# Gate and query projections: four jobs of four 128-row blocks with a 512-column product of high weights and split activations, in place of eight jobs of two blocks

## The reference

```
for l in (0, 1):                                   # two "mla" layers
    shift, scale, gate = split(silu(c) @ w_ada[l] + b_ada[l], 3)
    h = layernorm(x) * (1 + scale) + shift
    u_f, z_f, cq, ckv, k_r, z_a = split(h @ w_in[l])
    y_f = fourier_mix(u_f, w_fmix[l]) * silu(z_f)
    q  = rmsnorm(cq) @ w_q_b[l];  k, v = rmsnorm(ckv) @ w_kv_b[l];  rope on parts of q and k
    y_a = attention(q, k, v) * silu(z_a)           # 8 heads of 128
    x = layernorm(alpha * x + gate * (concat(y_f, y_a) @ w_out[l])) * g + b
# "even" layer
p_in, p_gate, dq, dk, dv, d_gate, iq, ik, iw = split(rms_norm(x) @ even_w_in)
score = sum_h relu(iq_h . ik) * iw_h;  the 64 best keys of each query are kept
x = x + concat(silu(p_gate) * pool(p_in), silu(d_gate) * attention(dq, dk, dv, kept keys)) @ even_w_out
# "odd" layer
q, k, v, gate = split(rms_norm(x) @ odd_w_in)      # 32 query heads of 64, a window of 128 tokens
x = x + (silu(gate) * window_attention(q, k, v)) @ odd_w_out
```

## Time and profile before

| what | value |
|---|---|
| device time, median of 3 runs | 1576.37 us |
| lowest and highest of the 3 runs | 1575.11, 1579.06 us |
| span of the profiled execution | 1576.4 us |
| PE busy | 1505.3 us, 95% |
| DVE busy | 1064.3 us, 68% |
| ACT busy | 708.5 us, 45% |
| mean granted TensorE clock, as a share of 2.4 GHz | 0.988 |
| transfers | 345.04 MB, mean 219 GB/s |

### The profile page before, as it was taken

How to read it: one execution, slowest core, us unless ns; L and a number is a source line. 1 busy time by engine, 2 the same in 40 slices (tenths; PEclk the granted TensorE clock), 3 DMA queues, 4 the chain that set the end, 5 groups by cost and what they waited for, 6 DMA issues and landing times.

```text
span 1576.4 us, 25483 instructions
## 1 busy us (share of the span) xinstructions
PE 1505.3 (95%) x10143; PEld 1332.0 (84%) x10143; DVE 1064.3 (68%) x1729; ACT 708.5 (45%) x1216; POOL 40.7 (3%) x58
## 2 busy tenths in 40 slices
PE   5999999989979999999979999999998999999999
PEld 3678789987869788998859998889987998888987
DVE  3348588889987667577576683795655657766653
ACT  2334244334445445444435444454444546655442
POOL 3000000000000000000000000010000000000000
PEclk9999999999989999999999999999999999999999
DMA  9998888998837555776645554456664554434673
GB/s 356 406 407 305 277 292 316 358 351 331 332 100 263 188 192 180 253 251 205 199 151 183 171 166 144 146 181 196 188 197 148 162 160 122 123 118 134 188 219 102
DMA packets 101422, 345.04 MB, mean 219 GB/s; under 512 B 11216, under 2 KB 21684, under 8 KB 100536
## 3 DMA queue, kind: packets, MB, share of 16 engines
q1 hardware_dynamic: 96888, 327.42, 61.7%
q0 software_dynamic: 4416, 16.00, 3.0%
HBM read 341.17 MB, written 2.20 MB: 218 GB/s over the span
## 4 chain that ended last, share of the span: by engine, by line
PE 72%; DVE 12%; DMA 7%; ACT 5%; issue 4%; SPq 1%; DVEq 0%; ACTq 0%
PE PM L1478 60%; PE PB L1478 7%; DMA stg<-in_w_in 5%; DVE wlo L2181 2%; ACT whi L1862 2%; DVE AC L2094 2%; ACT AR L1862 2%; PE PB L1713 1%; DVE X L2094 1%; DMA stg<-in_w_ada 1%; DMA stg<-in_w_out 1%; SPq L1387 1%; PE PB L1685 1%; DVE SM L2444 1%; PE PB L1788 1%
## 5 line engine op out<-in xcount | busy, mean ns | idle before, releaser
L2181 DVE TENSOR_TENSOR wlo<-stg,whi 128x1024 fp32r<-128x1024 f32 (+2 forms) x417 | 498.0, 1204 | 346.4 <-ACT whi L1862 344.4
L1862 ACT ACTIVATE whi<-stg 128x1024 fp32r<-128x1024 f32 (+2 forms) x417 | 430.0, 1039 | 440.7 <-PE PM L1478 336.0
L1478 PE MATMUL PM<-Hh,whi 128*128 128x256 f32 x1824 | 527.9, 292 | 12.6 <-DVE wlo L2181 8.5
L1478 PE MATMUL PM<-Hh,wlo 128*128 128x256 f32 x1776 | 500.1, 284 | 0.0
L1478 PE MATMUL PM<-Hl,whi 128*128 128x256 f32 x1824 | 496.5, 284 | 0.0
L1478 PEld LDWEIGHTS PM<-Hh,whi 128*128 128x128 f32 x1824 | 351.8, 193 | 31.2 <-issue 16.3
L1478 PEld LDWEIGHTS PM<-Hh,wlo 128*128 128x128 f32 x1776 | 342.8, 193 | 0.0
L1478 PEld LDWEIGHTS PM<-Hl,whi 128*128 128x128 f32 x1824 | 341.4, 192 | 0.8 <-issue 0.2
L1478 PE MATMUL PM<-whi,Hh 128*128 128x512 f32 (+1 forms) x576 | 224.8, 391 | 0.9 <-DVE wlo L2181 0.5
L1478 PE MATMUL PM<-wlo,Hh 128*128 128x512 f32 (+1 forms) x576 | 221.4, 385 | 0.0
L1478 PE MATMUL PM<-whi,Hl 128*128 128x512 f32 (+1 forms) x576 | 218.9, 385 | 0.0
(11 more groups left out here) (279 smaller groups left out, 1420.1 us busy)
## 6 DMA issues: line engine op xcount, KB each, us to landing
stg<-in_w_ada SPq DMA_DIRECT2D x163, 512.0 KB, 6.2
stg<-in_w_in SPq DMA_DIRECT2D x105, 512.0 KB, 5.3
stg<-in_even_w_in SPq DMA_DIRECT2D x80, 512.0 KB, 3.6
stg<-in_odd_w_in SPq DMA_DIRECT2D x72, 512.0 KB, 3.5
stg<-in_w_out SPq DMA_DIRECT2D x64, 512.0 KB, 4.0
stg<-in_even_w_out SPq DMA_DIRECT2D x32, 512.0 KB, 3.6
stg<-in_odd_w_out SPq DMA_DIRECT2D x32, 512.0 KB, 3.6
AR<-in_w_ada SPq DMA_DIRECT2D x29, 512.0 KB, 15.1
```

The lines of the kernel that those rows point to most:

```text
L1478: return e.matmul(out, l, r, start=start, stop=stop, skip_group_check=True)
L1862: return e.activation(out, x, f, **k)
L2181: e.tensor_tensor(wlo[s["slot"]][:, :, 0:n], stg[s["slot"]][:, :, 0:n], whi[s["hi"]][:, :, 0:n].bitcast(F32), ALU.subtract).then_inc(SEM[" ...
```

## The change

Gate groups, the query groups of the odd layer, those of the even layer and its second group of iq go from `group` to `wide`. `wide` makes four jobs of 256 output columns; a job holds four blocks of 128 rows. `Hh` and `Hl` of a block now lie side by side in `H2`, so that one matmul of 512 columns computes whi·Hh and whi·Hl into the two halves of a bank; wlo·Hh, with 256 columns, goes to the left half. A pair of banks then holds two blocks of columns, and its right halves have to be added to the left ones: ScalarE copies the two right halves to SBUF and VectorE adds. Of the handlers in the diff `wide` is TensorE's, the next three are ScalarE's and the last two VectorE's.

```diff
+    def wide(self, w, c0, post, pre=None):
+        g = {}
+        for q in range(4):
+            def body(job, q=q):
+                if q == 0:
+                    g["pair"], g["free"] = self.pairs.get()
+                tok = self.tick("mm")
+                self.step("wide", q=q, pair=g["pair"], free=g["free"] if q == 0 else (), split=job["split"], hi=job["hi"],
+                          slot=job["slot"], h=self.h[4 * q:4 * q + 4])
...
+            self.jobs.append(dict(mode="split", src=[(0, 256, w, 4 * q, c0)], n=512, mm=body, pre=pre if q == 0 else None,
+                                  post=done if q == 3 else None))
...
-    def gate_post(self, l, blocks):
+    def gate_post(self, l, b0):
...
-            for j in range(2):
-                b0 = blocks[2 * j]
-                self.drain(lambda: self.z[b0] is not None and self.z[b0 + 1] is not None)
-                i, ifree = self.now(self.tmps)
...
+            i, ifree = self.now(self.tmps)
+            r, total = self.tick("right_half"), self.tick("half_sum")
+            self.step("gate_sum", tmp=i, tfree=ifree, pair=pair, mm=mm, r=r)
+            self.round()
+            self.drain(lambda: self.z[b0] is not None and self.z[b0 + 1] is not None)
+            th, pr, y = self.tick("gate_tanh"), self.tick("gate_in"), self.tick("gate_y")
+            self.step("gate", b0=b0, tmp=i, pair=pair, total=total, th=th, pr=pr, z=[self.z[b0], self.z[b0 + 1]])
+            return [pr]
...
+    def two_out(self, pair, mm, dst, free):
+        r = self.tick("right_half")
+        self.step("two_out", pair=pair, mm=mm, dst=dst, free=free, r=r)
+        return self.tick("half_sum")
...
-        for j in range(4):
-            self.group([(w, j * 512, 512)], A4, q_post(j))
-        for j in range(4):
-            self.group([(w, 2560 + j * 512, 512)], A4, self.gate_post(l, list(range(4 * j, 4 * j + 4))))
+        for j in range(8):
+            self.wide(w, j * 256, q_post(j))
+        for g in range(8):
+            self.wide(w, 2560 + g * 256, self.gate_post(l, 2 * g))
...
+        H2 = sb("H2", [128, KT, 2, S], F32R)
+        Hh, Hl = H2[:, :, 0, :], H2[:, :, 1, :]
...
+                elif kind == "wide":
+                    q.wait_all(s["free"])
+                    q.wait_ge(s["split"])
+                    wh, wl = four(whi[s["hi"]]), four(wlo[s["slot"]])
+                    for kk in range(4):
+                        k = 4 * s["q"] + kk
+                        q.wait_ge(s["h"][kk])
+                        for j in range(2):
+                            b, cols = PM[2 * s["pair"] + j], slice(j * 128, j * 128 + 128)
+                            mm(b, wh[:, kk, cols], H2[:, k, :, :].rearrange("p t n -> p (t n)"), k == 0, False)
+                            ins = mm(b[:, 0:S], wl[:, kk, cols], Hh[:, k, :], False, k == KT - 1)
...
                 elif kind == "gate":
-                    q.wait_ge(s["mm"])
-                    q.wait_all(s["tfree"])
-                    act(TMP[s["tmp"]][:, :], (P0, P1)[s["j"]][:, :], ACT.Tanh, scale=0.5).then_inc(SEM["gate_tanh"], 1)
+                    q.wait_ge(s["total"])
+                    act(two(TMP[s["tmp"]][:, :]), halves(s, 0), ACT.Tanh, scale=0.5).then_inc(SEM["gate_tanh"], 1)
+                elif kind == "gate_sum":
+                    q.wait_ge(s["mm"])
+                    q.wait_all(s["tfree"])
+                    act(two(TMP[s["tmp"]][:, :]), halves(s, 1)).then_inc(SEM["right_half"], 1)
+                elif kind == "two_out":
+                    q.wait_ge(s["mm"])
+                    q.wait_all(s["free"])
+                    act(two(ar(s["dst"], 512)), halves(s, 1)).then_inc(SEM["right_half"], 1)
...
+                elif kind == "gate_sum":
+                    q.wait_ge(s["r"])
+                    q.wait_ge(s["mm"])
+                    e.tensor_tensor(halves(s, 0), halves(s, 0), two(TMP[s["tmp"]][:, :]), ALU.add).then_inc(SEM["half_sum"], 1)
+                elif kind == "two_out":
+                    x = two(ar(s["dst"], 512))
+                    q.wait_ge(s["r"])
+                    q.wait_ge(s["mm"])
+                    e.tensor_tensor(x, halves(s, 0), x, ALU.add).then_inc(SEM["half_sum"], 1)
```

More of the change, by code:

```diff
@@ L736, in heads @@
                 self.z[8 + h + n] = a
[L738 to L741, removed]
+        for g in range(8):
+            self.wide(w, (1024 if g < 4 else 1856) + g * 256, self.gate_post(l, 2 * g))
         return begin
@@ L868, in even, with iq_first @@
         qr = {}
+        def iq_first(pair, mm):
+            for m in range(2):
+                Tk["iq", m] = self.tick("iq_out")
+            self.step("iq_out", pair=pair, mm=mm, dst=IQ, free=tuple(arf))
+            return [Tk["iq", 1]]
         def iq_post(j):
             def post(pair, mm):
[L872 to L875, removed]
+                Tk["iq", j] = self.two_out(pair, mm, IQ + 2 * j * S, tuple(arf))
+                return [Tk["iq", j]]
             return post
-        self.group([(w, 4224, 512)], A4, iq_post(0))
+        self.group([(w, 4224, 512)], A4, iq_first)
         def ik_post(pair, mm):
@@ L900, in even @@
                    [unit("A", 0, 0, 0), unit("A", 1, 0, 128, 80)], ik_post)
[L901 removed]
+        for j in (2, 3):
+            self.wide(w, 4224 + j * 256, iq_post(j))
         def scores():
@@ L939, in post @@
             def post(pair, mm):
[L940 to L943, removed]
+                a = self.two_out(pair, mm, Q2 + 2 * j * S, tuple(arf))
+                Tk["q", 2 * j] = Tk["q", 2 * j + 1] = a
                 return [a]
             return post
-        for j in range(2):
-            self.group([(w, 2048 + j * 512, 512)], A4, q_post(j))
+        for j in range(4):
+            self.wide(w, 2048 + j * 256, q_post(j))
         def p_post(j):
@@ L984, in even @@
             self.group([(w, j * 512, 512)], B2, p_post(j), pre=q_rinv if j == 0 else None)
[L985 to L988, removed]
+        for g in range(8):
+            self.wide(w, (1024 if g < 4 else 2176) + g * 256, self.gate_post(l, 2 * g))
         return begin
@@ L1015, in post @@
             def post(pair, mm):
[L1016 to L1021, removed]
+                a = self.two_out(pair, mm, IQ + 2 * j * S, tuple(arf))
+                Tk["q", 2 * j] = Tk["q", 2 * j + 1] = a
+                if j % 2:
+                    g = j // 2
+                    self.start(self.head_rinv(4, IQ + 4 * g * S, {("q", k): Tk["q", 4 * g + k] for k in range(4)}, 80 + 16 * g, qr[g]))
+                    self.start(heads(g))
                 return [a]
```

51 lines of the change are left out of this document (31 added, 20 removed).

## The result

The changed kernel takes 1595.81 us (median of 4 runs, 1592.07 to 1598.74). The kernel before, run beside it on the same chip, takes 1576.45 us (4 runs, 1575.11 to 1579.06). The ratio is 1.0115, 95% interval 1.0095 to 1.0135: slower, by 19.4 us at the medians. The forecast was 1573.6 us, its range 1560 to 1587. The profiled execution of the changed kernel took 1592.07 us, of which its span is 1590.3; in every execution that gives both, 1.75 to 2.24 us lie outside the span. So the span before, 1576.4 us, does not equal the median because nothing lies outside of it: that agreement was chance, worth some 2 us.

A forecast was written before the change was run, and what follows sets the result against it. PE was taken to bound the clean gate stretches, VectorE and loads layer 0, VectorE and ScalarE much of the odd attention, the even layer between. 1576.4 - 12.9 (PE gain) + 10.1 (costs) = 1573.6 us, range 1560 to 1587.

The forecast's parts named there:

- What is added: All layers: costs of the added copies, additions and waits, 10.1 us in sum.
- What bounds the kernel: PE alone in layer 1's gates; VectorE and loads in layer 0; VectorE and ScalarE mostly in odd attention; even layer between.
- That part once per three matmuls: Wide streams: 13.3 ns beside a matmul's columns saved once per three matmuls, 0.42 us a piece.
- A gate piece costs VectorE 0.69 of work plus about 0.7 of standing still = 1.4 us: Each gate piece: VectorE's addition plus its wait for the tanh, 1.4 us.
- Its copies cost nothing as long as the next `whi` is not late: ScalarE, everywhere: it has room, so added copies cost nothing, else 0.6 us each.
- I take the middle, 6.4: Layer 0: seven gate pieces cost between 3.1 and 9.8 us, depending on VectorE's usable idle time; 6.4 us taken.
- Odd attention: ... 2.8 us: Odd layer's attention: three gates cost 4.2 us, of which the chain's non-PE share, 2/3, passes on: 2.8 us.
- 2 x 1.4 x 1/3 = 0.9: Even layer: two gates cost 0.9 us; its six other additions nothing, or 1.4 us.
- I price this at nothing, the work being the same: Gate pieces: one more call of `round` each makes attention steps slightly denser; no cost.
- VectorE's round trip multiplies in layer 0: Rival, 20%: layer 0's standing delays slot releases and loads, a gate costs 1.4 + 2.35 us; 1593 us, or 1585.
- The pair of banks is not free in time: Rival, 5%: in attention stretches, queue waits hold the banks, 15 mixed pieces with 1 us each; 1589 us.
- A matmul's fixed part is not saved: Rival, 6%: the mixed stream keeps four fifths of the 13.3 ns, the gain is 2.6 us; 1583.9 us.

The follow-up runs named there:

- experiment 1: The changed kernel without the extra call of round between the sum and the gate; 1591.05 us.
- experiment 3: The changed kernel without extra round, gates' copies and all additions, so right halves are never added; 1567.02 us.
- experiment 5: The changed kernel without extra round; in each gate piece the tanh and two VectorE steps behind it issued one weight job later; 1575.02 us.
- 13: As experiment 5, with the 14 queries' additions also issued one weight job after their copies; 1571.03 us.
- form 11: The changed kernel without extra round; copy, addition and tanh at once, only the two VectorE steps behind the tanh one job later; 1589.56 us.
- experiment 6: The changed kernel without extra round and without the gates' 32 ScalarE copies; additions add the tile's old content; 1590.54 us.
- Form 9: The changed kernel without extra round; the whole gate (copy, addition, tanh, two steps) issued in one piece, one job later; 1586.10 us.
- 14: As 13, but layer 0's gates stay in groups of 512 columns as before; 1572.16 us.
- experiment 4: Only the 14 query and iq pieces wide; gates in groups as in the kernel before, no extra round; 1577.11 us.
- 12: As form (10), with the 14 queries' additions also issued one job after their copies; 1575.92 us.
- experiment 2: The kernel before with one more call of round after the fourth and eighth job of each gate group, nothing wide; 1583.84 us.
- form (10): As experiment 5, cut once more: gate copy at the piece's end, addition one job later, tanh and two steps another job later; 1580.68 us.

## Why the prediction was wrong

The step that failed is "What is added", the sum of costs: 10.1 us were said, and the runs show 24.0 for the sums and 4.8 for the extra round that was priced at nothing. It priced a gate piece by VectorE's time, scaled that with the share of the chain that is not PE's, and put ScalarE's waits and the queries' additions at nothing. Moving the same instructions behind the next job brought back 16.0 us in the gates and 4.0 in the queries, so most of the cost was one of order. The gain, 12.9 us, was too high by 3.5.

The start of the last gate step (`Z<-TMP,Z`) of each layer, from the timelines of the profiled executions:

| | layer 0 | layer 1 | even | odd |
|---|---|---|---|---|
| before | 366.56 | 732.64 | 1134.81 | 1498.62 |
| changed | 368.72 | 731.94 | 1139.40 | 1512.32 |
| 1, no round | 369.84 | 734.01 | 1138.57 | 1511.30 |
| 3, no sums | 360.05 | 721.23 | 1122.35 | 1482.44 |
| 5, tanh later | 365.89 | 728.98 | 1130.78 | 1496.64 |
| 13, both later | 362.12 | 726.33 | 1128.45 | 1491.60 |

The row of experiment 1 less that of experiment 3 is what the sums cost up to each place: 9.8, 12.8, 16.2, 28.9 us, so 9.8, 3.0, 3.4 and 12.6 by layer (28.9 in these two executions, 24.0 at the medians, since the profiled execution of experiment 3 took 1563.94 us, 3.1 less than its median; each entry good to 2 or 3 us).

- **What bounds the kernel:** right. PE in layer 1, VectorE and ScalarE in the odd layer's attention, a mixture in layer 0. Layer 1, from the last gate step of layer 0 to its own, shortened from 366.1 to 363.2 us, where 3.4 was said.
- **"That part once per three matmuls", 0.42 us a piece:** half right. The pair takes 0.353 us, 0.22 us a piece. What failed here is the assumption that a matmul of each length keeps the pace that it has among its own kind. An estimate from the 2.5 ns a matmul of the Trainium skill (TensorE: Matmul & The Clock Gate, "Wait — 56ns, not 53.3ns?") is 3.7 us for all pieces; experiment 3 gave 9.4, between that and 19.4. The total gain of 12.9 us came as near to the 9.4 as it did by luck, because two errors met: too much for each piece, and no gain at all for layer 0, which had one (360.05 against 366.56 us at its end).
- **"A gate piece costs VectorE 0.69 of work plus about 0.7 of standing still = 1.4 us":** the row shows exactly this (0.69 and 0.66), and in layer 0 it is the account that fits: form 11, which takes VectorE's standing away and leaves ScalarE's, is there as good as form 5. In the odd layer it does not fit, since form 11 gives nothing there.
- **"Its copies cost nothing as long as the next `whi` is not late":** the copies did cost nothing that shows (6), but ScalarE's wait for the addition, 32.0 us in all, has no term. In layer 0 taking VectorE's standing away was enough (11), and in three pieces of seven the load was late anyway; in the odd layer the place of the tanh behind the addition cost (9, 11).
- **Layer 0, "I take the middle, 6.4":** 9.8 measured, the upper bound. Not because VectorE is full: experiment 5 has the same VectorE work and is 4.0 us earlier at its end (near the limit of what a single execution tells), with more work done by both engines in the same 114 us, and 14 shows that the additions there do no net harm.
- **"Odd attention: ... 2.8 us":** the largest miss. The odd layer costs 12.6 us. Its share was worked out by scaling VectorE's 1.4 us with the chain. From the even layer's last gate step to the odd one's experiment 1 takes 372.7 us and form 5 365.9, so 6.9 of the 12.6 are the gates' order; that a wait is passed on there with all that is queued behind it is my reading and was not taken apart. The clock is a small part of the 12.6: in the stretch from 1298 us it is 0.99 in experiment 1 and 1.00 in experiment 3. It weighs more in the changed kernel (0.97), but form 5 is not free of it either:

```profile
1370.00:1410.00 40.00, 37.14 (x249) 29.53 (x248) 30.94 (x78) 23.95 (x67) 0.00 (x0) 1.00 0.32 107
1410.00:1452.00 42.00, 40.14 (x244) 32.56 (x243) 30.17 (x66) 27.01 (x70) 0.00 (x0) 0.96 0.40 128
```

- **The clock over the whole run** had no term. The median granted clock is 0.9815 in the changed kernel, 0.982 in experiment 1, 0.9875 in 5, 0.989 in 13 and 0.987 to 0.988 in the kernel before. The difference between 1 and 5 is at most some 9 us of full clock by my estimate (0.0055 x 1590). How much of the 16.0 us came by this way, PE standing and then running at the lower level, stays open.
- **Even layer, "2 x 1.4 x 1/3 = 0.9", "the query additions nothing":** 3.4 us measured, and the queries lost the 3.1 us that their pieces give (experiment 4); 4.0 to 4.8 us come back when their addition no longer stands for its copy (12, 13).
- **The extra `round`, "I price this at nothing, the work being the same":** wrong. 7.4 us alone in the kernel before, 4.8 us at the medians in the changed one. The same work in another order is not the same.
- **The rivals:** "VectorE's round trip multiplies in layer 0" (20%) had a mechanism near to what happened, and its 1593 us is near the 1595.81 measured; but that is luck, for its place was wrong. At the end of layer 0 the changed kernel is 2.2 us late, at the end of the even layer 4.6 and at the end of the odd one 13.7. "The pair of banks is not free in time" did not occur: PE's idle time is put down to `wlo` and to attention tiles. "A matmul's fixed part is not saved" is half true and would have given 1583.9.

So the sum was 1576.4 - 12.9 + 10.1. With measured terms it is 1576.4 - 9.4 + 24.0 + 4.8 = 1595.8 us; these terms are differences of the runs themselves, so that they add up confirms nothing.

## What to carry to other kernels

When an edit puts a step of engine B between two steps of engine A, price A's wait and B's, not only B's work: each stands until the other's queue reaches the step, and what is queued behind is late, if it could have gone ahead. Look at what stands behind: in layer 0 the next `whi` often had no load yet, and ScalarE's wait was free then. Issue the second step of A later, behind the work that can go ahead; here that, with VectorE's steps behind it, turned 1591 us into 1575, and with the queries' additions put off too, the same matmul saving became a gain, 1571 us. An extra call that hands out work early should be priced as a change of order, not at nothing. And check a cause found in totals stage by stage: by the totals ScalarE's wait looked like most of it, by layers it did not.

## What the runs showed that was not expected

- A 512-column and a 256-column matmul in turn take 0.353 us for the pair. From streams of one kind, 0.2268 and 0.1200, one would say 0.3468.
- Changing only the time of issue of 32 attention steps costs 7.4 us (experiment 2), more than the 32 copies and VectorE's waits for them, which cost nothing measurable (experiment 6).
- Taking a wait away can cost: form (10) has VectorE's 14.1 us of waiting for the copy reduced to 0.0 and is 5.7 us slower than form 5. This stays unexplained.
- Form 9, with ScalarE standing 14.6 us for the additions of the odd layer, goes through its gates as fast as form 5, where it stands 5.1 us; form 11, with 12.5 us, is 7 to 8 us slower.
